# Order of the gated scores, of one copy, one read-out and six modulation rows in a two-block transformer kernel

## The reference, cut to what matters

```
mod  = silu(c) @ w_ada + b_ada                 # 6 x 1024, the "modulation"
proj = modulate(x, norm1_g, shift1, scale1) @ w_in
log_a = log_sigmoid(a_lr @ w_alpha + b_alpha) / 16
b = cumsum(log_a) inside each chunk of 64 tokens, 4 heads of 64
scores[t,s] = sum_k q[t,k] k[s,k] exp(b[t,k] - b[s,k]),  s <= t     (per head and chunk)
o_intra = scores @ v;   state = exp(b_last) * state + (k * exp(b_last - b))^T v
o_inter = (q * exp(b)) @ state
o_swa = banded softmax attention with sinks, 8 heads, then rms_norm
x = x + gate1 * (concat(norm(o_gla) * silu(r), o_swa) @ w_out)
```

## Time and profile before

| | us |
|---|---|
| median of three runs | 1647.15 |
| lowest, highest | 1644.25, 1650.11 |
| the profiled execution: its time | 1646.64 |
| its span | 1645.0 |
| TensorE matmul busy | 1582.4 (96%) |
| VectorE busy | 1067.8 (65%) |
| ScalarE busy | 840.1 (51%) |
| mean granted TensorE clock | 0.984 of full speed |

### The profile page before, as it was taken

The page is one execution under the profiler, slowest core; times in us unless marked ns, Lnnn a source line. Parts: engine busy times, 40 slices in busy tenths (PEclk is TensorE's granted clock), DMA queues, the critical chain, the costliest instruction groups (busy, mean ns, idle before and its releaser), DMA issues.

```text
span 1645.0 us, 33139 instructions
## 1 busy us (share of the span) xinstructions
PE 1582.4 (96%) x10878; PEld 1438.6 (87%) x10878; DVE 1067.8 (65%) x2417; ACT 840.1 (51%) x1808; POOL 494.1 (30%) x489
## 2 busy tenths in 40 slices
PE   6999999999999999999999999899999999999998
PEld 4788899999999999787877877789999888889997
DVE  5675589739889886555555574756555654455555
ACT  3334555655555555554555553555455525745554
POOL 4111779888777774001000003311000101300000
PEclk9997999999999999999999999899999999999999
DMA  8861345554444445557555554127555742145554
GB/s 334 294 239 65 118 153 173 178 174 165 161 161 163 163 159 174 189 192 286 192 191 191 191 190 158 52 103 270 186 183 181 254 141 91 49 157 181 189 181 152
DMA packets 81474, 288.72 MB, mean 176 GB/s; under 512 B 10160, under 2 KB 11488, under 8 KB 81280
## 3 DMA queue, kind: packets, MB, share of 16 engines
q1 hardware_dynamic: 70144, 248.91, 45.2%
q0 software_dynamic: 9936, 35.79, 5.8%
q10 hardware_dynamic: 1328, 3.15, 0.5%
HBM read 285.19 MB, written 2.62 MB: 175 GB/s over the span
## 4 chain that ended last, share of the span: by engine, by line
PE 86%; DVE 5%; ACT 3%; issue 2%; POOL 2%; DMA 1%; DVEq 0%; ACTq 0%; POOLq 0%; SPq 0%
PE pu L657 13%; PE pu L658 13%; PE pu L659 13%; PE pacc L714 9%; PE pacc L716 8%; PE pacc L715 8%; PE pu L625 2%; PE pu L637 2%; PE pacc L1070 2%; PE pacc L657 2%; PE pacc L658 2%; PE pacc L659 2%; POOL ring_lo L436 1%; DVE ring_lo L436 1%; PE pacc L774 1%
## 5 line engine op out<-in xcount | busy, mean ns | idle before, releaser
L429 ACT ACTIVATE ring_hi<-ring 128x512 fp32r<-128x512 f32 x880 | 505.0, 622 | 373.1 <-PE pacc L716 194.9
L436 DVE TENSOR_TENSOR ring_lo<-ring,ring_hi 128x512 fp32r<-128x512 f32 x592 | 385.4, 693 | 333.9 <-ACT ring_hi L429 333.4
L657 PE MATMUL pu<-Xh,ring_hi 128*128 128x256 f32 x1472 | 425.6, 289 | 12.5 <-DVE Xl L1881 3.2
L658 PE MATMUL pu<-Xl,ring_hi 128*128 128x256 f32 x1472 | 418.3, 284 | 0.0
L659 PE MATMUL pu<-Xh,ring_lo 128*128 128x256 f32 x1472 | 418.1, 284 | 0.0
L436 POOL TENSOR_TENSOR ring_lo<-ring,ring_hi 128x512 fp32r<-128x512 f32 x288 | 371.1, 1311 | 89.9 <-ACT ring_hi L429 89.1
L657 PEld LDWEIGHTS pu<-Xh,ring_hi 128*128 128x128 f32 x1472 | 284.1, 193 | 21.1 <-issue 13.5
L658 PEld LDWEIGHTS pu<-Xl,ring_hi 128*128 128x128 f32 x1472 | 284.5, 193 | 0.2
L659 PEld LDWEIGHTS pu<-Xh,ring_lo 128*128 128x128 f32 x1472 | 284.2, 193 | 0.0
L714 PE MATMUL pacc<-ring_hi,vh 128*128 128x512 f32 x512 | 201.0, 393 | 3.8 <-DVE vl L2324 3.7
L716 PE MATMUL pacc<-ring_lo,vh 128*128 128x512 f32 x512 | 200.4, 391 | 0.0
(11 more groups left out here) (405 smaller groups left out, 2429.2 us busy)
## 6 DMA issues: line engine op xcount, KB each, us to landing
ring<-in_weights SPq DMA_DIRECT2D x472, 512.0 KB, 3.4
big<-in_ada POOLq DMA_DIRECT2D x40, 512.0 KB, 7.3
big<-in_w POOLq DMA_DIRECT2D x12, 512.0 KB, 7.5
bias_row<-big ACTq DMA_DIRECT2D x1, 1536.0 KB, 6.8
XT<-in_xT ACTq DMA_DIRECT2D x1, 1024.0 KB, 8.3
scr<-in_ada POOLq DMA_DIRECT2D x2, 512.0 KB, 12.3
tk<-in_ada POOLq DMA_DIRECT2D x2, 512.0 KB, 14.1
early_h<-in_ada POOLq DMA_DIRECT2D x2, 512.0 KB, 16.1
```

Source lines behind the costliest of these rows:

```text
L429: nc.scalar.activation(ring_hi[:, n % 2, half], ring[:, n % RING, half], ACT.Copy).then_inc(s["split_hi"], 1)
L436: api.tensor_tensor(ring_lo[:, n % RING, half], ring[:, n % RING, half], ring_hi[:, n % 2, half], ALU.subtract).then_inc(s[LOW[name][0]], 1)
L657: mm(out, ring_hi[:, n % 2, w], xh, start=start, stop=False, skip_group_check=True)
L658: mm(out, ring_hi[:, n % 2, w], xl, start=False, stop=False, skip_group_check=True)
```

## The change

It has four parts. `gla_scores` takes a pair of heads and runs over sub-blocks, then token tiles, heads and chunks, so that four matmuls in a row go to four different quarters of the array; the same matmuls are issued in the same two places. `swa_sums` stands behind slot 17 and no longer inside it. On ScalarE the read-out of slot 0 is taken out of the loop and put between the copy of the gate's input and the wait for the gate's product, and the copy to `klT` is put ahead of the high part of `w_out`'s slot 1. On VectorE the six modulation rows 16 to 21 go ahead of the wait for `la_parts`, so ahead of the whole decay computation.

```diff
-            def gla_scores(heads):
-
-                for h in heads:
-                    for c in range(NCHUNK):
-                        for i in range(NSUB):
-                            rows = slice((c % 2) * 64, (c % 2) * 64 + 64)
-                            col = T + ((h // 2) * TT + c // 2) * CHUNK + i * SUB
-                            t0 = c * CHUNK
-                            last = mm((pm, pn)[h % 2][rows, col:col + SUB],
...
+            def gla_scores(hp):
+
+                for i in range(NSUB):
+                    for tt in range(TT):
+                        for h in (2 * hp, 2 * hp + 1):
+                            for c in (2 * tt, 2 * tt + 1):
+                                rows = slice((c % 2) * 64, (c % 2) * 64 + 64)
+                                col = T + (hp * TT + tt) * CHUNK + i * SUB
+                                t0 = c * CHUNK
+                                last = mm((pm, pn)[h % 2][rows, col:col + SUB],
+                                          kp[keys_at(h), i, hp * T + t0:hp * T + t0 + CHUNK],
+                                          qp[keys_at(h), hp, t0 + i * SUB:t0 + (i + 1) * SUB], start=True, stop=True)
                 return last
...
-                    gla_scores((0, 1))
+                    gla_scores(0)
...
-            gla_scores((2, 3)).then_inc(s["gla_scores"], 1)
+                if i == 16:
+                    gla_scores(1).then_inc(s["gla_scores"], 1)
             swa_step(swa_steps)
...
-            n, e = SLOT["w_in"] + 17, USE["w_in"] + 17
-            wait_slot(n)
-            pe.wait_ge(s["evacs"], e - 1)
-            for c in range(C):
-                if c == 6:
-                    swa_sums()
-                last = mm(entry(e), slot(n)[:, c * P:(c + 1) * P], HTf[:, c, :], start=(c == 0), stop=(c == C - 1))
-            last.then_inc(s["slots_used"], 1)
-
+            project(SLOT["w_in"] + 17, USE["w_in"] + 17, HTf)
+            swa_sums()
...
             f(alr[0:16, :], pm[0:16, 0:T], ACT.Copy).then_inc(s["alr_copied"], 1)
+            evac(SLOT["w_in"], qs[:, 0, :], entry(USE["w_in"]), scale=float(SD) ** -0.5)
             act.wait_ge(s["z_psum"], 1)
...
+                if i == 0:
+                    continue
                 if i < 4:
                     evac(n_slot, qs[:, i, :], src, scale=float(SD) ** -0.5)
...
-            split_high(act, "w_out", 1)
             act.wait_ge(s["kl_psum"], 1)
             f(klT, paccf[:, 512:1024].rearrange("p (a b c) -> p a b c", a=HP, b=TT), ACT.Copy).then_inc(s["kl_copied"], 1)
+            split_high(act, "w_out", 1)
...
+            modulation(2 * C, 6)
             dve.wait_ge(s["la_parts"], 1)
             step(v.scalar_tensor_tensor(la, zb, 0.0, zln, ALU.min, ALU.subtract))
...
             v.tensor_scalar(kp, kp, 80.0 * GATE_TEMP, None, ALU.min).then_inc(s["ex_ready"], 1)
-            modulation(2 * C, 6)
```

More of the change, by code:

```diff
@@ L870, in keys_at @@
                 return slice((h % 2) * 64, (h % 2) * 64 + 64)
-            def gla_scores(heads):
-                for h in heads:
-                    for c in range(NCHUNK):
-                        for i in range(NSUB):
-                            rows = slice((c % 2) * 64, (c % 2) * 64 + 64)
-                            col = T + ((h // 2) * TT + c // 2) * CHUNK + i * SUB
-                            t0 = c * CHUNK
-                            last = mm((pm, pn)[h % 2][rows, col:col + SUB],
-                                      kp[keys_at(h), i, (h // 2) * T + t0:(h // 2) * T + t0 + CHUNK],
-                                      qp[keys_at(h), h // 2, t0 + i * SUB:t0 + (i + 1) * SUB], start=True, stop=True)
+            def gla_scores(hp):
[9 more added lines that the diff above has]
+                                          qp[keys_at(h), hp, t0 + i * SUB:t0 + (i + 1) * SUB], start=True, stop=True)
                 return last
```

## The result

The changed kernel takes 1631.59 us (median of four runs, 1630.49 to 1632.02) against 1645.70 (median of four, 1643.30 to 1650.11) for the kernel before, run beside it: a ratio of 0.9914, 95% interval 0.9895 to 0.9933, so 14.1 us less. The profiled executions stand at 1631.73 and 1646.64, 14.9 us apart. The forecast was 1634.7, in a range of 1630 to 1642.

The account below looks back on a forecast made before the run. TensorE, with 86% of the chain that ended last, was taken as the bound, along with its waits and clock falls. Terms 3.75 + 0 + 0.6 + 8.15 + 0 = 12.5 us gave 1634.7 us, range 1630 to 1642.

Parts of the forecast that it names:

- no fall at all: Rival: shorter score blocks keep the clock up too, so neither fall comes; 15.4 us gained, 1631.7 us; chance 0.12.
- Read-out of slot 0: ScalarE reads slot 0 out early, so slot 2 loses its wait (2.71 us) and the clock stays full (1.04): 3.75 us.
- Six rows: Six modulation rows ahead of the decay on VectorE: no gain or cost, 0 us; bounds nothing to 3 us lost.
- nothing gained, as VectorE had no wait behind these rows that TensorE feels: Upper bound of the six rows' move on VectorE: no gain possible from it.
- Gated scores: Two score blocks over the array's quarters, at 30 to 32 ns an instruction: 0.6 us gained, bounds 0 and 2.4.
- The clock: First fall, in the second score block, stays at the same price; no second fall taken: 0 us, bound 2.9 gained.
- I let the first fall stand: The fall in the second gated-score block stays, as some 5.6 us of low activity remain: gain 0, bound 2.9.
- Slot 17 whole, keys copied first: From S, the end of swa_sums, to L985: wait for ScalarE goes, full clock, L985 at S + 10.45; 8.15 us gained.
- Behind the change: The work from L985 to the end of the span: unchanged, 0 us.
- All that follows keeps its distances from L985: Work behind the sums of the gated output shifts with L985 unchanged, adding 0 us.
- Quarters in series: Rival: score matmuls in different quarters run one after the other at 0.21 us each; 10 us slower, 1657; chance 0.03.
- late rows: Rival: rows 20 and 21 arrive late, the decay ends after 62 us and slot 8 waits; 1641 us; chance 0.09.

Follow-up runs that it names:

- undo_rows: The changed kernel with the six modulation rows put back behind the decay on VectorE: 1632.55 us (1631.20 to 1634.47).
- undo_quarters: The changed kernel with the gated scores in the old order (head, chunk, sub-block): 1636.50 us (1633.22 to 1638.60).
- only_quarters: The kernel before with the new order of the gated scores alone: 1638.51 us (1635.36 to 1645.81), ratio 0.9955 to the kernel before.
- scores_twice: The changed kernel with each block of gated scores issued twice, in the new order: 1637.22 us (1634.23 to 1640.00).
- late_filled: The changed kernel with swa_sums inside slot 17, the keys' copy behind the split, and 29 zero matmuls in place of 10 ahead of the state products: 1633.73 us.
- undo_copy: The changed kernel with the keys' copy (to klT) behind the split again, swa_sums staying behind slot 17: 1631.15 us (1630.48 to 1632.74).
- undo_late: The changed kernel with swa_sums inside slot 17 and the keys' copy behind the split, as before: 1640.91 us, eleven runs.
- col_halves: The changed kernel with gated scores over head, sub-block, tile and chunk, so consecutive matmuls alternate between column halves only: 1631.49 us, single run.

## Why the prediction came out as it did

The time lay inside the range, but the case that came true was the one given 0.12, no fall at all, priced at 1631.7. That the forecast came within some 3 us has a part of luck: in the traces the stage gained 17.67 us and not 12.5, and 2.8 were given back behind it. Step by step:

- *Read-out of slot 0*, 3.75 forecast: 4.34 in the traces. No wait is left and the clock is full, as said; a slot with no attention work beside it has a pitch of 13.92 / 4 = 3.48 us, where I had used 3.65. So slot 2 had started 2.95 us late, not 2.71, and the fallen clock had cost 11.83 - 10.44 = 1.39, not 1.04. That this fall is a sure consequence of the wait was wrong: three other traces have the wait and a clock of 1.00 behind it. So this term belongs to the profiled execution of the kernel before, and to the pair's difference, more than to the change.
- *Six rows*, 0 forecast: right as a sum, and the decay ended at 59.4, inside the time I gave it. The step "nothing gained, as VectorE had no wait behind these rows that TensorE feels" failed: it looked at the old schedule. At the new one the rows would have been late, as undo_rows shows: 2.01 us of wait in its trace, 1 us in the median.
- *Gated scores*, 0.6 forecast: mis-sized. Block and following wait give 5.67 - 4.34 = 1.33 and, for the second, 6.77 - 5.67 = 1.10 (to 114.83 from 121.60): 2.4, at my upper bound. Some 0.4 of it is the fallen clock in the second block before, which took 121.60 - 118.83 = 2.77 us where the first took 2.38, so the order itself is worth 2.0. The pitch was 17 ns and not 30. The rest of the second block's gain is held up by ScalarE's copies, as said; that wait is 0.56 us.
- *The clock*, 0 forecast: this step failed. "I let the first fall stand" rested on a stretch of 5.6 us of small matmuls. With blocks of 1.06 us it is 115.42 - 110.92 = 4.5 us instead of 7.4, and the clock held. Last products and slot 17 took 0.46 + 2.39 = 2.85 us less, against a bound of 2.9. undo_quarters and only_quarters show that this belongs to the order of the scores. Whether the length of the stretch or the pitch within it decides is open: scores_twice was to tell, and could not.
- *Slot 17 whole, keys copied first*, 8.15 forecast: 17.67 - 9.62 = 8.05. Root at S + 0.04, copy ending at S + 1.07, wait for VectorE 0.44 instead of 0.8, L980 at S + 10.4 against 10.45. I had no fall here, which late_filled confirms as a matter of idle time. With the sums behind slot 17 the copy's move is worth nothing (undo_copy); what it is worth without them was not run.
- *Behind the change*, 0 forecast: 2.8 us given back in the profiled pair, 2.2 of them to falls of the clock in the two places above. From L980 (or its like) to the end of the span nine traces of these kernels take between 1496.1 us (the kernel before) and 1500.9 (undo_late), and undo_copy, which differs from the changed kernel by one copy, takes 1497.2 where the changed kernel takes 1498.8. So differences of this size come from one execution to the next, and the 2.8 need no cause in the change.

4.34 + 2.43 + 2.85 + 8.05 - 2.8 = 14.9. "All that follows keeps its distances from L985" was the step that erred on the other side, and it hid part of the two mis-sized terms. Quarters in series and late rows did not happen.

## What to carry to other kernels

A wait of some two microseconds on TensorE with small matmuls behind it can cost three to four times its length (2.25 us cost 7.9 in undo_late's trace), as these then run at 1.2 GHz; take such a wait out, or cover it with matmuls on zeros, before making the work around it quicker. Where contraction and output are 64 wide, order the matmuls so that neighbours differ in row half and column half. Price a moved step against the schedule that the other edits make, not against the old one. Do not take a fallen clock in one profile for a part of the kernel: look at a second execution first.

## What the runs showed of the hardware

- The pitch of 64 x 64 x 16 float32 matmul instructions at a granted clock of 1.00 is 37 ns (undo_quarters), 28 (col_halves), 21 (row_halves) or 17 (changed kernel) by order alone.
- The clock fell to 0.50 at about 115 us (undo_quarters) and 115.8 us (col_halves) with TensorE busy without a gap, behind or within blocks of small matmuls; it held in the eight traces with blocks of 1.06 us.
- A fall followed by small matmuls lasted long: 125.7 to 139 us in undo_late, 134 to 148 in the kernel before. Behind the wait of slot 2 in the kernel before, with matmuls of the whole array, it lasted from 49 to 52.4 us.
- The same kernel spreads over 10 us (undo_late 1632.96 to 1642.49), and the run's mean granted clock goes with the times: 0.990 for the shortest, 0.983 for the longest. Covering the wait with zero matmuls narrowed the spread as well as the median (late_filled, 1631.26 to 1634.99).
- When the score instructions were doubled at 17 ns each, TensorE stood for 2.51 us with nothing that the trace names as its release. What it waited for stays open.
